# Delta projections and early merge gates from seven block products per pair of tiles, joined on GpSimd

## What is computed

```python
h = rms_norm(x, norm_mix)
proj = h @ w_in                                   # 512 x 1024 @ 1024 x IN_TOTAL
qkv_a, qkv_b, z_b, beta_b, alpha_b, gate_a, gate_b = split_columns(proj, IN_WIDTHS)
...
qkv_b = causal_short_conv(qkv_b, conv_w)          # 4 taps per channel, then SiLU
qb = l2_norm(qb) * 128 ** -0.5 ; kb = l2_norm(kb)
o_b = gated_delta_rule(qb, kb, vb, beta, g)       # per chunk: (I + A)^-1, u, w, state update
o_b = rms_norm(o_b, dn_out_norm) * silu(z_b)
merged = sigmoid(gate_a) * (o_a @ w_branch_a) + sigmoid(gate_b) * (o_b @ w_branch_b)
x = x + merged @ w_out
```

## Time and profile before

| | |
|---|---|
| median of 3 runs | 2806.08 us (2804.14 to 2807.78) |
| the profiled execution, its own time | 2807.2 us |
| its span, first to last instruction | 2805.2 us |
| TensorE clock granted, mean | 0.981 |
| PE busy | 2725.2 us, 97% |
| DVE, ACT, POOL busy | 1310.3, 588.4, 60.8 us |
| the decay and delta stages | about 377 to 873 us of the span |

### The profile page before, as it was taken

The page is one execution under the profiler, slowest core; times in us unless marked ns, Lnnn a source line. Parts: engine busy times, 40 slices in busy tenths (PEclk is TensorE's granted clock), DMA queues, the critical chain, the costliest instruction groups (busy, mean ns, idle before and its releaser), DMA issues.

```text
span 2805.2 us, 30376 instructions
## 1 busy us (share of the span) xinstructions
PE 2725.2 (97%) x11882; PEld 1761.6 (63%) x11882; DVE 1310.3 (47%) x2849; ACT 588.4 (21%) x1068; POOL 60.8 (2%) x52
## 2 busy tenths in 40 slices
PE   8999999999999999999999998999999999999998
PEld 4777647676674445444444445578884474788887
DVE  2255555556542012000012576467666673777743
ACT  1155541212301001110011124222220012112201
POOL 0222100000000000000000000000000000000000
PEclk9999999999999998999999997999999999999999
DMA  4211110101012221344423210122223211222222
GB/s 184 75 46 61 46 60 31 46 31 46 30 46 105 75 84 40 120 165 169 161 105 112 75 60 1 60 83 91 91 89 107 105 49 60 81 85 90 91 90 90
DMA packets 32487, 226.89 MB, mean 81 GB/s; under 512 B 3552, under 2 KB 4192, under 8 KB 6112
## 3 DMA queue, kind: packets, MB, share of 16 engines
q1 hardware_dynamic: 30384, 219.50, 22.1%
q10 hardware_dynamic: 1968, 5.51, 0.5%
HBM read 222.90 MB, written 2.10 MB: 80 GB/s over the span
## 4 chain that ended last, share of the span: by engine, by line
PE 92%; DVE 4%; ACT 3%; issue 1%; DMA 0%; ACTq 0%; DVEq 0%
PE psum L400 90%; DVE work L2466 1%; PE psum L894 0%; DVE hT L572 0%; ACT work L960 0%; ACT work L963 0%; PE psum L1216 0%; PE psum L2330 0%; PE psum L2029 0%; PE psum L1841 0%; DVE work L1041 0%; ACT work L611 0%; DMA mixT<-x_dram 0%; ACT mixT L749 0%; ACT work L972 0%
## 5 line engine op out<-in xcount | busy, mean ns | idle before, releaser
L400 PE MATMUL psum<-hT,ring 128*128 128x512 f32 (+2 forms) x3152 | 793.4, 428 | 9.4 <-DVE work L769 2.3
L400 PEld LDWEIGHTS psum<-hT,ring 128*128 128x128 f32 (+1 forms) x3152 | 423.8, 165 | 274.5 <-issue 239.7
L400 PE MATMUL psum<-work,ring 128*128 128x512 f32 (+1 forms) x1208 | 420.1, 499 | 8.7 <-DVE work L2528 3.9
L400 PEld LDWEIGHTS psum<-work,ring 128*128 128x128 f32 x1208 | 228.9, 190 | 184.7 <-issue 158.0
L400 PEld LDWEIGHTS psum<-work 128*128 128x128 f32 (+2 forms) x2390 | 276.5, 178 | 105.2 <-issue 65.5
L400 PE MATMUL psum<-work 128*128 128x128 f32 (+7 forms) x2390 | 327.3, 290 | 13.1 <-ACT work L2428 9.9
L400 PE MATMUL psum<-work,mixT 128*128 128x256 f32 (+2 forms) x1332 | 290.9, 381 | 2.7 <-DVE work L1938 1.5
L400 PEld LDWEIGHTS psum<-work,mixT 128*128 128x128 f32 (+1 forms) x1332 | 232.7, 183 | 50.3 <-issue 16.9
L400 PE MATMUL psum<-ring,work 128*128 (+1 forms) x568 | 248.7, 596 | 2.2 <-issue 1.9
L400 PEld LDWEIGHTS psum<-ring,work 128*128 128x128 f32 x568 | 107.2, 191 | 133.6 <-issue 130.2
L2792 DVE SCALAR_TENSOR_TENSOR work<-work,vec 128x512 f32<-128x512 f32 x176 | 125.7, 749 | 69.5 <-ACT work L2727 69.5
(11 more groups left out here) (427 smaller groups left out, 2428.6 us busy)
## 6 DMA issues: line engine op xcount, KB each, us to landing
ring<-stream_dram SPq DMA_DIRECT2D x204, 1024.0 KB, 4.7
con<-consts_dram SPq DMA_DIRECT2D x1, 2953.0 KB, 13.4
mixT<-x_dram ACTq DMA_DIRECT2D x4, 512.0 KB, 6.3
work<-x_dram ACTq DMA_DIRECT2D x4, 512.0 KB, 5.0
out_dram<-mixT SPq DMA_DIRECT2D x4, 512.0 KB, 3.7
work<-p_dram ACTq DMA_DIRECT2D x1, 512.0 KB, 3.9
con<-ssm_dram ACTq DMA_DIRECT2D x1, 512.0 KB, 3.6
vec<-vecs_dram SPq DMA_DIRECT2D x1, 378.0 KB, 5.7
```

The lines of the kernel that those rows point to most:

```text
L400: ins = self.eng.matmul(out, lhsT, rhs, start=start, stop=stop)
```

## The change

Nineteen fills of the projection queue, all but the first (K0 and V0 of pair 0), are made from seven parts of four products of 256 columns, 28 in all, in place of 16 of 512 columns. The parts use the `in_sums` that lie in `xT` from the attention stage. GpSimd forms four sums of weight quadrants in the ring slot itself (`split_sums_pool`, `split_joins_pool`) and makes the seven additions that join the parts. As GpSimd doesn't read PSUM, ACT first copies the parts out: two copies of 512 columns and three of 256 per fill (`split_first_act` to `split_last_act`), in place of two copies of 512. SiLU of z and sigmoid of the gates become an instruction of their own on two tiles (`gated_act`). The filters move: Q0 to the opening, Q1 to level 1, K0 and V0 to levels 4 and 5, K1 and V1 to chunks 1 to 4. The k-q product moves from the opening to the end of level 2, and what DVE makes of it (`attnT`, `qdT`) to level 3. `prod` takes the place of `ksq` instead of `kT`. The diff is cut and some bodies are written on one line; its comments number the copies, sums and joins as the text does.

```diff
+        PLAIN, HALVES = 2, 28
+        def part_at(g, p):   return 7 * (QK_FILLS + g) + p + 1
+        def sum_at(g, n):    return 4 * (QK_FILLS + g) + n
+        def copy_at(g, n):   return 2 * QK_FILLS + 5 * g + n
+        class SplitProjection:
+            def some(self, e, n):
+                for n in range(self.n, self.n + n):
+                    g, at = divmod(n, HALVES)
+                    if at == 0:
+                        e.eng.wait_ge(S[e.landing()], e.landed())
+                        fill_at["split%d" % g] = e.c["fill"].n
+                        self.w = e.slot(ring)
+                    self.half(e, g, *divmod(at, 4))
+            def half(self, e, g, p, k):
+                if k == 0:
+                    if p == 0 and g == 0:  e.eng.wait_ge(S["proj_free"], PLAIN)
+                    if p == 0 and g >= 1:  e.eng.wait_ge(S["part_out"], copy_at(g - 1, 4))
+                    if p == 2:
+                        if g >= 1:         e.eng.wait_ge(S["part_out"], copy_at(g - 1, 5))
+                        e.eng.wait_ge(S["slot_sum"], sum_at(g, 1))
+                    if p == 3:             e.eng.wait_ge(S["slot_sum"], sum_at(g, 2))
+                    if p == 4:             e.eng.wait_ge(S["part_out"], copy_at(g, 1))
+                    if p == 5:             e.eng.wait_ge(S["slot_sum"], sum_at(g, 3))
+                    if p == 6:
+                        e.eng.wait_ge(S["part_out"], copy_at(g, 2))
+                        e.eng.wait_ge(S["slot_sum"], sum_at(g, 4))
+                weights, moving = ((blk(w, k), hT[:, k, early]), (blk(w, 4 + k), hT[:, 4 + k, early]),
+                                   (blk(w, k), in_sums[:, 2, k, :]), (blk(w, 8 + k), in_sums[:, 0, k, :]),
+                                   (blk(w, 12 + k), in_sums[:, 3, k, :]), (blk(w, 8 + k), in_sums[:, 1, k, :]),
+                                   (blk(w, 4 + k), hT[:, 4 + k, late]))[p]
+        def split_first_act(e, i, t):     # copy 1: 512 columns
+            if g >= 1: e.eng.wait_ge(S["proj_add"], 7 * g)
+            e.eng.wait_ge(S["part"], part_at(g, 1))
+            nc.scalar.activation(split_two, acc[:, 0, :], ACT.Copy).then_inc(S["part_out"], 1)
+        def split_second_act(e, i, t):    # copy 2: 512 columns, after part 3
+            tile_empty(e, i, t + 1)
+            e.eng.wait_ge(S["part"], part_at(g, 3))
+            nc.scalar.activation(split_tile(i, t + 1), acc[:, 1, :], ACT.Copy).then_inc(S["part_out"], 1)
+        def split_third_act(e, i, t):     # copies 3 and 4: 256 columns each, after part 5
+        def split_last_act(e, i, t):      # copy 5: 256 columns, after part 6 and join 2
+        def split_sums_pool(e, i, t):
+            e.eng.wait_ge(S["part"], part_at(g, 0))
+            nc.gpsimd.tensor_tensor(a11, a11, a21, ALU.subtract).then_inc(S["slot_sum"], 1)
+            e.eng.wait_ge(S["slot_sum"], sum_at(g, 1))
+            nc.gpsimd.tensor_tensor(a21, a21, a22, ALU.add).then_inc(S["slot_sum"], 1)
+        def split_joins_pool(e, i, t):
+            e.eng.wait_ge(S["part_out"], copy_at(g, 1))
+            nc.gpsimd.tensor_tensor(t00, one, two, add).then_inc(S["proj_add"], 1)          # join 1
+            e.eng.wait_ge(S["part"], part_at(g, 3))
+            nc.gpsimd.tensor_tensor(a21, a22, a11, ALU.subtract).then_inc(S["slot_sum"], 1) # sum 3
+            nc.gpsimd.tensor_tensor(a12, a12, a21, ALU.subtract).then_inc(S["slot_sum"], 1) # sum 4
+            e.eng.wait_ge(S["part_out"], copy_at(g, 4))
+            nc.gpsimd.tensor_tensor(one, one, two, add).then_inc(S["proj_add"], 1)          # joins 2 to 6
...
+            e.eng.wait_ge(S["part_out"], copy_at(g, 5))
+            nc.gpsimd.tensor_tensor(t01, two, one, add).then_inc(S["proj_add"], 1)          # join 7
         def decay_pe(e):
-            proj.some(e, 2 * DC)
+            split.some(e, HALVES)
             four_turned(e, H[0].A, delta_rows).then_inc(S["decay_pe"], 1)
-            proj.some(e, 2 * DC)
+            split.some(e, HALVES)
         def decay_act(e):
...
+            split_first_act(e, 0, K1)
             tapped_act(e, 0, K0)
-            tile_out_act(e, 0, K1)
+            split_second_act(e, 0, K1)
+            split_third_act(e, 0, K1)
             tapped_act(e, 0, V0)
+            split_last_act(e, 0, K1)
...
         def chain_pe(e, i):      # opening: 4, 4, 4, 2, 2 products become 7, 7, 7, 7; levels: 3 and 3 become
                                  # 5 or 6 and 5; after w: 4 and 4; chunks: 2 + 1 per step become 4 + 2
-            proj.some(e, 2)
-            for s, h in enumerate(H):      # qk, in the opening
-                four(e, h.B, lambda b: (blk(d.kT[:, s, :], b), blk(d.qT[:, s, :], b))).then_inc(S["opened"], 1)
-            proj.some(e, 2)
+            split.some(e, 7)
...
+                if n == 2:                 # the same products after level 2
         def merge_pe(e):
-            e.eng.wait_ge(S["proj_free"], PROJ * PAIRS + 2 * EARLY)
+            e.eng.wait_ge(S["part_out"], copy_at(split_fill(PAIRS, 6), 5))
```

More of the change, by code:

```diff
@@ new lines, in gated_act @@
+        def gated_act(e, i, t):
+            g = split_fill(i, t)
+            e.eng.wait_ge(S["proj_add"], 7 * g + 7)
+            if i == PAIRS:
+                two, func = (D_SETS[0].qT, D_SETS[0].vT, D_SETS[0].ksq, D_SETS[0].kT)[t // 2], ACT.Sigmoid
+            else:
+                two, func = pair_set(i).zs, ACT.Silu
+            nc.scalar.activation(two, two, func).then_inc(S["proj_free"], 1)
+        def split_sums_pool(e, i, t):
+            g = split_fill(i, t)
+            w = ring[:, fill_at["split%d" % g] % RING, :]
+            a11, a12, a21, a22 = (w[:, 512 * q:512 * q + 512] for q in range(4))
+            e.eng.wait_ge(S["part"], part_at(g, 0))
+            nc.gpsimd.tensor_tensor(a11, a11, a21, ALU.subtract).then_inc(S["slot_sum"], 1)
+            e.eng.wait_ge(S["slot_sum"], sum_at(g, 1))
+            nc.gpsimd.tensor_tensor(a21, a21, a22, ALU.add).then_inc(S["slot_sum"], 1)
@@ L1241, in program, with projections_pool @@
+        def projections_pool(e):
+            for i in range(PAIRS + 1):
+                for t in range(0, PROJ, 2):
+                    if (i, t) != (0, 0):
+                        split_sums_pool(e, i, t)
+                        split_joins_pool(e, i, t)
+        proj, split = Projection(), SplitProjection()
         DECAY_STEP = {"rows_zero": 1, "minus_abs": 2, "rows": 3, "cols": 4, "alpha_beta": 1, "rows_turned": 2,
@@ L1404, in chain_pe @@
                 e.mm(h.C, row(0, 8, 2 * i + s), delta_rows[0:8, :]).then_inc(S["opened"], 1)
-            proj.some(e, 4)
+            split.some(e, 7)
             for s, h in enumerate(H):
@@ L1440, in chain_pe @@
                     four(e, h.C, lambda b: (blk(d.prod[:, s, :], b), blk(h.xinvT, b))).then_inc(S["prod_xt"], 1)
-                proj.some(e, 3)
+                split.some(e, 5)
+                if n == 2:
+                    for s, h in enumerate(H):
+                        e.eng.wait_ge(S["silu"], TAPPED * i + (Q0, Q1)[s] + 1)
+                        if i > 0:
+                            e.eng.wait_ge(S["o_ln"], nth(i - 1, s))
+                        four(e, h.B, lambda b: (blk(d.kT[:, s, :], b), blk(d.qT[:, s, :], b))).then_inc(S["opened"], 1)
             for s, h in enumerate(H):
@@ L1446, in chain_pe @@
                 four(e, h.C, lambda b: (blk(h.k_bg, b), blk(h.xinvT, b))).then_inc(S["w"], 1)
-            proj.some(e, 4)
+            split.some(e, 4)
             for c in range(T // CH):
@@ L1460, in chain_pe @@
                     if c < 7:
-                        proj.some(e, 1)
+                        split.some(e, 2)
                 for s, h in enumerate(H):
@@ L1472, in chain_pe @@
                 if c < 7:
-                    proj.some(e, 2 if c == 0 else 1)
+                    split.some(e, 4 if c == 0 else 2)
         def delta_pe(e):
```

218 lines of the change are left out of this document (148 added, 70 removed).

## The result

The changed kernel takes 2781.2 us (median of 4 runs, 2780.5 to 2782.0), the kernel before in the same session 2805.7 (4 runs, 2804.1 to 2807.8): a ratio of 0.992, 95% interval 0.990 to 0.993. The forecast was 2782, its range 2775 to 2798. The profiled execution took 2780.5 us, its span 2778.4.

The account below looks back on a forecast made before the run. PE, busy 97% of the span, was taken to bound the kernel. The 17 fills outside decay -28.0, decay +2.4 and openings +1.8 give -23.8 from 2807.2; less 1.1, 2782 us, range 2775 to 2798.

Parts of the forecast that it names:

- A fill gets 1.65 us shorter: PE's products: a fill drops from 13.73 to 12.08 us, 19 fills save 31.3 us, 6.6 of it a pair.
- Decay, +3.4 up to `k_sum`: Decay stage: two fills save 3.3 us, against stalls of 5.2 and 1.2 and 0.3 for sums meeting filters.
- The second stall: Second fill of decay: PE waits 1.2 us for sum 1 (0.7 to 4.6), plus 0.3 for sums 3 and 4.
- the first stall: First split fill of decay: PE waits 5.2 us (2.7 to 5.9) at part 6 for ACT's copy 2, queued behind K0's filter.
- Pair 0's stall for L1506 goes: Pair 0's decay row: its 0.99 us wait behind SiLU and square of Q0 disappears, -1.0 us.
- Openings, 0.45 a pair: End of each pair's opening: one join delays DVE's L1609, PE waits 0.45 us longer, 1.8 us over four pairs.
- Levels and chunks, 0: Levels and chunks of the pairs: no loss, at worst 1 us for each of five levels.
- The end, -1.65: Last fill, ahead of merge: 1.6 us saved, with no added wait for copies or the last tile's sigmoid.
- the three signs of being wrong: Gaps at borders of 256-column parts, joins over 1 us, or PE waiting for DVE inside levels or chunks.
- The likeliest case: Whole kernel: the forecast itself, 2782 us, 0.9% faster, chance 0.50.
- waits in every pair: The 17 fills outside decay: ACT's order loses 9.5 us, 2792 us; with a late level 2802; chance 0.23.
- GpSimd makes DVE the bound: Pairs: GpSimd's hold delays DVE 13 us a pair, total 2833 us, gain gone from 6.6 a pair; chance 0.07.

Follow-up runs that it names:

- plain_decay: Changed kernel with both fills of the decay stage made of eight products a tile again, the 17 others still split: 2779.3 us, ratio 0.990 to the kernel before.
- square_first: Changed kernel with the sigmoid of gates 4 and 5 moved behind the last square root on ACT: 2777.2 us, ratio 0.990 to the kernel before.
- half_decay: Changed kernel with only the decay's second fill split, its first plain, and the sigmoid of gates 4 and 5 behind the last root: 2764.1 and 2766.0 us, ratio 0.986.
- copy_first: Changed kernel with ACT's copies 2 to 4 of the first split fill ahead of K0's SiLU and square: 2783.0 us, ratio 0.992 to the kernel before.
- kq_early: Changed kernel with the k-q product back in the opening and Q1's filter back beside Q0's on DVE: 2801.5 us, ratio 0.9985 to the kernel before.
- more_reads: Changed kernel with eight unused GpSimd adds of 128 columns behind the last join of fills 2 to 17: 2795.4 us, ratio 0.996 to the kernel before.
- own_pad: copy_first plus a pad of its own for pair 0's V1, and copy 5 ahead of V0's `tapped_act`: 2779.5 us, ratio 0.991 to the kernel before.
- half_only: half_decay with the sigmoid of gates 4 and 5 left where the changed kernel has it: 2776.4 us, ratio 0.989 to the kernel before.
- half_later: half_decay with two extra products of 512 columns in the decay's first fill, their result overwritten: 2771.8 us, ratio 0.988 to the kernel before.

## Why the prediction was right

The start of merge moved by -22.19 us in the trace, 0.3 of them ahead of the decay stage, where nothing was changed; so the stages of the forecast gave -21.9, where its terms give -23.8. The total moved by -24.5 by the medians. Step by step:

- **A fill gets 1.65 us shorter: right.** plain_decay against the changed kernel isolates no clean fill, but the end in square_first is 1.61 us under that of the kernel before (16.54 against 18.15), and half_decay's decay is 1.54 under 28.01. Inside the pairs 6.6 were forecast and 6.47 came, 0.12 of the difference being the opening. Parts of 256 columns show no gap over 0.1 us at their borders where nothing holds them.
- **Decay, +3.4 up to `k_sum`: measured +3.64**, made differently. The stall is 4.34, not 5.2. The second stall is 0.17, not 1.2 + 0.3, since PE, slowed by the clock, came to part 2 only 7.4 us after the end of the first stall (forecast 5.6), when sum 1 was done (7.2, forecast 6.8; it had waited for part 0, no longer for the joins). And the fallen clock added 1.8. Idle time is counted from a modelled end of a matmul; from start to start the stalls are 4.5 and 0.4, and with 1.8 for the clock and 0.3 of slower starts at the borders of parts they are 7.0 us, which less 3.3 is the 3.64 to within 0.1. So two errors met: stalls that were forecast too long, and a clock that had no term. The mechanism of the first stall was incomplete: the prediction named the ACT queue alone, and copy_first shows that the pad would hold copy 2 by itself to within 1.2 us. The turns of DVE and GpSimd are there as forecast. By the Trainium skill, "SBUF — State Buffer", section "Who interferes with whom", their shared ports are an exclusive lock, and a DVE instruction with two SBUF inputs contends with a GpSimd instruction that reads SBUF; the rows agree, with three multiply-adds in 4.16 us beside two sums and in 2.33 alone. The three instructions that were late here have one input. The same section says of copies and `tensor_scalar` that they can contend when they run in a mode with two ports; that they waited for turns the rows show (1.06, 1.38 and 0.88 us), in which mode they ran they don't.
- **Pair 0's stall for L1506 goes: right.** Pair 0 is 7.5 us shorter, forecast 6.6 + 1.0 - 0.45.
- **Openings, 0.45 a pair: measured 0.12.** The next two periods are 6.47 us shorter, forecast 6.15. One join got in between, as forecast, but it held only the first of the two subtractions of L1787 (1.82 us for both, 1.29 before).
- **Levels and chunks, 0: right**, by the chain of 81.79 us without a wait. But the room is narrow: kq_early and more_reads show what 2 us more at one place cost, 3 us a pair.
- **The end, -1.65: wrong, measured +0.09.** The step "I went through the copies of a pair against the parts that wait for them" looked at what waits for the copies, and not at the square that waits behind a sigmoid which now waits for GpSimd. PE's longer wait (2.42 for 1.11) made the last pair 5.17 us shorter instead of 6.47 like the others, and the fallen clock in `out_sum` (5.2 for 3.5) ate the 1.65 of the last fill. square_first gives both back.
- **Everything behind merge, 0: not held in the trace** (-4.6 in the span's unchanged part against the profiled execution before, -2.3 by medians: 24.5 less 22.2). It is of the size that the clock's course moves this part by itself: in the traces of all these kernels it takes from 1918.0 to 1932.1 us, with the same 7974 PE records. That it covered the 1.9 us too little before merge is luck, and so is how near 2781.2 lies to 2782.

Of the three signs of being wrong, no gaps over 0.1 us at borders of parts and no waits for DVE inside levels or chunks appeared; but 21 of the 133 joins took over 1 us (up to 1.18, median 0.73). What they cost PE inside the pairs is the 0.12 us of the opening.

The likeliest case came in; "waits in every pair" and "GpSimd makes DVE the bound" did not, but kq_early is what the latter looks like: 3.1 to 6.0 of the 6.6 us a pair that would have decided it.

The version that beats both kernels is half_decay: 2764 to 2766 us, 1.4% under the kernel before.

## What to carry to other kernels

When work moves to a slow helper engine, list for every instruction that now waits for it what stands behind it in its own queue; the two losses here (a copy behind a filter, a square behind a sigmoid) were both such. Use fewer products only where the helpers' work has room: in this kernel's pairs, not in the first fill of the decay, where it falls on DVE's unbroken run. And treat a gain of a few microseconds in the total as unproven until the stage itself shows it: compare starts on the timeline, since the unchanged stages behind merge differed by up to 14 us between these traces, with the clock.

## What the runs showed of the hardware

- After PE waits of 2.1 to 4.3 us the granted clock fell to the 1.2 GHz level for a few microseconds in some places (means of 0.50 at 395 us, 0.58 at 833, 0.66 at 541 in kq_early), and at `out_sum` of own_pad and half_only it didn't after the same 2.4 us. One and the same wait can do either: in kq_early the waits of 2.07 and 0.67 us brought it down in pairs 0 and 1 and not in 2 and 3, in more_reads the 2.42 us in pair 0 and in no other. After 1.1 us at `out_sum` it never did, in six traces.
- With 1.9 us more of work before merge the mean granted clock of the whole execution was 0.981 (all six executions of half_later), where it was 0.985 or 0.986 (six of eight of half_decay), and the total rose by 6 to 8 us, the 1.9 included. The kernel before shows the same spread without any change: in that session one execution of eleven ran at 0.986 and took 2793.8 us, the median 2807.3 at 0.982.
- GpSimd's add of 256 columns takes 0.64 to 0.73 us alone, 0.91 to 1.18 beside DVE, one of 512 columns 1.27 and up to 1.79. Eight of 128 columns, each waiting for the one before, take 4.2 us, beside two-input work on DVE 5.0; eight memsets of 128 columns 2.05.
- A DVE instruction with one input can wait for a GpSimd sum too: a copy of 8x8 took 1.06 us instead of 0.16.
